# Attention's preparation in another order: keys by halves of the sequence, queries split ahead of the gathers, constants behind the first maximum

## The chip, the cores and the metric

The kernel runs on one core of a Trainium2 chip as a single program. The metric is the time of one execution on the device in microseconds (us); the lower the better. The engines of the core are named as the profile names them: PE (TensorE, matrix products and transposes), DVE (VectorE), ACT (ScalarE), POOL (GpSimd) and SP (SyncE, which here only issues DMA transfers). Each engine runs its own list of instructions strictly in order and waits on semaphores for the others.

## The reference, cut to what matters

The program is one step of a hybrid decoder layer: RMS norm, one input projection, attention beside a state-space model, an output projection and a convolutional feed-forward block. It is run for a prompt of 1024 positions and for 8 sample rows with 2048 cached positions each. The change touches the attention alone. For the prompt (8 heads, 2 key heads, head width 64, query blocks of 128) and the sample rows, three branches are computed and added with gates:

```python
s_c = jnp.einsum('bqhgd,bnhd->bqhgn', q, kv_c[:, :, 0]) * scale      # compressed keys
...
o_s = jnp.einsum('bqhgm,bqhmd->bqhgd', masked_softmax(s_s, m_s), v_s)  # selected blocks
...
o_w = jnp.einsum('bqhgw,bwhd->bqhgd', masked_softmax(s_w, m_w), v_w)   # window of 512
g = jax.nn.sigmoid(gate_logits)
return g[..., 0:1] * o_c + g[..., 1:2] * o_s + g[..., 2:3] * o_w
```

## The kernel before, in words

The program is a row of stages; `stage_attend` stands between `stage_compress` (compressed keys and values) and the state-space stage. It works through 16 groups: query block `i` (128 queries) times key head. For each group PE first makes scores only to find their maxima (a "look", lines 1242 and 1245, 1233 and 1234 for the compressed branch); DVE reduces them (`top`, line 1617), PE turns the maxima (line 1254), and DVE writes them into the lower rows of `q2` (line 1634), so that the real score (lines 1275, 1278, 1279) comes out with its maximum already taken off. ACT takes the exponential (line 1467), PE multiplies by the values (line 1293), ACT, PE and DVE bring the product back and weigh it with `gates` ("out"). Scores are computed in two parts: queries and keys are split into a rounded upper part (`q_up`, `k_up`, `kT` rows 0 to 63) and a rest (`q2` on POOL, line 1547; `kT` rows 64 to 127 on DVE, line 1577); `k2` holds the keys again (POOL, line 1495) and constants in its lower half (DVE, line 1597).

The order of the steps of all groups, with the steps of the sample rows woven in, is one list, `ORDER`, which every engine walks through; it is the same before and after. At its beginning stand both first splits, the three looks of group 0, their `merge` and `turn`, and then the first score. Twenty-odd steps later comes `("cmp weigh", 0)`, the first step of the sample rows that needs `grow`.

Ahead of that list each engine has a preparation of its own. PE turns keys and compressed values (lines 1194, 1197, 1200), then waits for the split keys, the compressed keys (`kc`, `kc2`) and the kept values. ACT computes `exp` of the gate logits, splits the four key quarters `c` (two branches by two halves of the sequence) and then splits the queries of groups 0 and 1. POOL copies the keys into `k2`, makes masks, issues the first five gathers (`fetch`, line 1530) and subtracts the queries' upper parts. DVE copies the values, makes `grow`, `rows4` and `qsm`, computes `gates` from the logits, and only then subtracts the keys' upper parts, sets constants and prepares `kc`.

`grow` are the gates of the 8 sample rows, one row of 3 numbers for each head of each sample row, brought by 64 small DMAs of SP. SP may start them when DVE has announced the gates (`gated`, second increment):

```python
sp.wait_ge(gated, 2)
sp.wait_ge(lanes_made, 1)
for b in range(NB):
    for h in range(NH):
        r = LANES * (b % (NB // 2)) + h
        sp.dma_start(k.grow[r:r + 1, b // (NB // 2), :], k.gates[b:b + 1, NT, 3 * h:3 * h + 3]).then_inc(grow_in, 16)
```

DVE waits for all of them in `cmp weigh` of the first half of the sample rows, ahead of lines 1604 and 1605:

```python
elif kind == "cmp weigh":
    dve.wait_ge(s_powered, order_of["cmp max", g] + 1)
    if g == 0:
        dve.wait_ge(grow_in, 16 * NB * NH)
    weight(0, g)
```

PE needs what DVE writes there in `cmp turn` (line 1322).

Of the kernel before, what the change touches and what calls it, by code (L numbers as in the profile page):

```python
# [949 lines left out]
def stage_attend(nc, k):  # L950
# [64 lines left out]
    k_split = nc.alloc_semaphore("k_split")  # L1015
# [33 lines left out]
    k.attend_sems = [v_turned, v_kept, gated, k_turned, k_upper, k_split, k2_rows, k2_const, kc_upper, kc_split, minus_made, masked,  # L1049
# [115 lines left out]
    TURN, ROW = 2, 3  # L1165

    with nc.Block() as block:
# [21 lines left out]
        def _(pe):  # L1189
            for c in range(4):  # L1190
                src = KVW * (1 + c // 2)
                for a in range(4):
                    t = 4 * (c % 2) + a
                    mm = pe.transpose(k.ps[:, c, a * P:a * P + P], k.kv[:, t, src:src + P], k.ident[:])
                mm.then_inc(k_turned, 1)
# [7 lines left out]
            pe.wait_ge(k_split, 16)  # L1203
            pe.wait_ge(kc_split, 3)
            pe.wait_ge(v_kept, 2)
# [16 lines left out]
            for step in ORDER:  # L1222
                kind, g, *rest = step
                i, kvh = GROUPS[min(g, len(GROUPS) - 1)]
                if kind == "look":
                    br, h0, nh, b_lo, b_hi = rest
                    if h0 == 0 and br == 0:
                        pe.wait_ge(q_upper, 2 * g + 2)
                    wait_bank(pe, looks)
# [27 lines left out]
                elif kind == "score":  # L1257
# [3 lines left out]
                    if br == SEL and b == 0:  # L1261

                        pe.wait_ge(q_rest, g + 1)
                        pe.wait_ge(reduced, looks_before[g] + 1)
                        if g == 0:
                            pe.wait_ge(k2_rows, 8)
                            pe.wait_ge(k2_const, 1)
                            pe.wait_ge(masked, 4)
# [12 lines left out]
                elif kind == "value":  # L1281
# [6 lines left out]
                    else:  # L1288
                        pe.wait_ge(v_set, 1)
                        pe.wait_ge(v_kept, 1)  # L1290
# [16 lines left out]
                elif kind == "cmp score":  # L1307
                    to_row(step)
                    if g == 0:
                        pe.wait_ge(s_const, 1)  # L1310
                    for bb in range(NH2):
# [78 lines left out]
        def _(act):  # L1390
            act.activation(k.glog[:, 0:NT], k.kv[:, 0:NT, 3 * KVW:], ACT.Exp, scale=-1.0)
            act.activation(k.glog[0:NB, NT], k.kv[0:NB, NT, 3 * KVW:], ACT.Exp, scale=-1.0).then_inc(gated, 1)
            for c in range(4):
                act.wait_ge(k_turned, c + 1)
                act.activation(k.k_up[:, c], k.ps[:, c, :], ACT.Copy).then_inc(k_upper, 1)
                act.wait_ge(k_upper, c + 1)
                for kvh in range(NKV):
                    act.activation(k.kT[0:HD, c // 2, kvh, 4 * P * (c % 2):4 * P * (c % 2 + 1)], k.k_up[HD * kvh:HD * (kvh + 1), c],
                                   ACT.Copy).then_inc(k_split, 1)
# [6 lines left out]
            def upper(g):  # L1406
# [4 lines left out]
                for half in range(2):  # L1411
                    act.activation(k.q_up[HD * half:HD * half + HD, g % 2], q_of(g), ACT.Copy).then_inc(q_upper, 1)
            scores = values = 0
            for step in ORDER:
                kind, g, *rest = step
                if kind == "split":
                    upper(g)
# [40 lines left out]
                elif kind == "score":  # L1458
# [6 lines left out]
                    if scores == 0:  # L1465
                        act.wait_ge(k2_rows, 8)
                    act.activation(probs[br][:, b - first].rearrange("p h q -> p (h q)"), k.ps[:, 4 + scores % 2, :], ACT.Exp,
# [12 lines left out]
        def _(pool):  # L1480
# [7 lines left out]
            pool.wait_ge(minus_made, 3)  # L1488
            pool.wait_ge(*k.rows_stored)
            pool.wait_ge(v_set, 1)  # L1490
            pool.wait_ge(gated, 1)
            for c in range(4):
                pool.wait_ge(k_upper, c + 1)
                for kvh in range(NKV):
                    pool.tensor_copy(k.k2[0:HD, c // 2, kvh, 4 * P * (c % 2):4 * P * (c % 2 + 1)],
                                     k.k_up[HD * kvh:HD * (kvh + 1), c].bitcast(F32)).then_inc(k2_rows, 1)
            pool.wait_ge(k2_rows, 8)
# [41 lines left out]
            for kind, g, *rest in ORDER:  # L1539
                if kind == "unit":  # L1540
                    fetch(g)
                elif kind == "split":
                    pool.wait_ge(q_upper, 2 * g + 2)
                    if g >= 2:

                        pool.wait_ge(scored, scores_to(g - 2, CMP))
                    pool.tensor_tensor(k.q2[0:HD, g % 2], q_of(g), k.q_up[0:HD, g % 2].bitcast(F32), ALU.subtract  # L1547
                                       ).then_inc(q_rest, 1)

        @block.vector  # L1550
        def _(dve):
            link = Link(dve, a_link)
            for br in range(2):
                v = KVW * (1 + br) + P
                dve.tensor_copy(k.v1[:, :, br, :, 0:HD], k.kv[:, 0:NT, v:v + P].rearrange("p t (h d) -> p t h d", h=NKV))
            dve.wait_ge(k.u_spilled, 16)
            dve.memset(k.grow[:], 0.0).then_inc(lanes_made, 1)
            for f in range(4):
                ins = dve.tensor_scalar(k.rows4[:, f], k.rows_of[:], 4.0, float(f), ALU.mult, ALU.add)
            ins.then_inc(lanes_made, 1)  # L1560
# [990 lines left out]
```

## Time and profile before

| what | value |
|---|---|
| time, median of 3 runs | 1937.73 us (1937.3 to 1938.95) |
| the profiled execution's own time | 1938.17 us |
| its span, first to last instruction | 1936.5 us |
| mean granted clock of PE | 0.951 |
| busy: PE, DVE, ACT, POOL | 92%, 47%, 29%, 16% of the span |

The attention stage lies at 384 to some 830 us of the span. Shares of busy time say which engine has most to do over the whole program; the change lies in the stage's first 50 us, so the rows that matter are the order of time and the waits there. "Idle before" in brackets is the time that an engine stood still ahead of an instruction, and behind the arrow what ended it.

### The profile page before, as it was taken

The page shows a single profiled execution, that of the slowest core. Times are in us where ns is not written, and L with a number is a line of the kernel's source. Part 1 is how long each engine was busy: PE and PEld are TensorE (multiplying, and loading weights), DVE is VectorE, ACT ScalarE, POOL GpSimd, SP SyncE. Part 2 cuts the span into 40 slices and gives each one's busy share as a digit, 9 for nine tenths or more (in the row PEclk, how much of TensorE's full clock was granted, in tenths as well). Part 3 has the DMA queues.
Part 4 walks back from the last instruction along what each step waited for, and adds up shares of the span by engine and source line. Part 5 has one row for each costly group of instructions (what it writes and reads, how often), then busy time and mean ns, then how long its engine had stood idle before and what let it go on. Part 6 is the DMA issues. An engine that isn't in the chain of part 4 may idle for free. (4 is left out here: it accounts for less than half of the span.)

```text
span 1936.5 us, 27098 instructions
## 1 busy us (share of the span) xinstructions
PE 1773.3 (92%) x10876; PEld 1496.6 (77%) x10876; DVE 908.3 (47%) x1408; ACT 565.1 (29%) x872; POOL 311.8 (16%) x273
## 2 busy tenths in 40 slices
PE   5999999949989999858879799999999999999988
PEld 4655989936555554456579789999999999999977
DVE  3366127755554444154031265555555555555454
ACT  4000115534443443212031242222322222232222
POOL 0000100032123111210021022222212222222110
PEclk8999999969999999968989799999999999999999
DMA  6222434312325233661020311111211211112102
GB/s 253 50 73 109 164 111 180 126 55 66 109 68 194 65 103 138 206 171 43 0 87 1 77 34 33 45 53 32 65 32 32 65 32 56 41 32 65 32 12 93
DMA packets 90956, 155.15 MB, mean 80 GB/s; under 512 B 15574, under 2 KB 68350, under 8 KB 88526
## 3 DMA queue, kind: packets, MB, share of 16 engines
q1 hardware_dynamic: 76976, 92.77, 14.8%
q0 software_dynamic: 13056, 59.77, 9.2%
q10 hardware_dynamic: 848, 1.54, 0.3%
q8 instruction: 54, 0.88, 0.2%
q14 instruction: 22, 0.18, 0.0%
HBM read 133.61 MB, written 24.83 MB: 82 GB/s over the span
## 5 line engine op out<-in xcount | busy, mean ns | idle before, releaser
L2240 PE MATMUL ps<-h_up,w_split 128*128 128x344 f32 x2112 | 403.5, 323 | 9.2 <-DVE h_rest L2410 7.3
L2419 DVE TENSOR_TENSOR xT<-ps,xT 128x1032 f32<-128x1032 f32 x176 | 216.9, 1233 | 326.5 <-PE ps L2240 326.5
L2240 PEld LDWEIGHTS ps<-h_up,w_split 128*128 128x128 f32 x2112 | 344.1, 189 | 20.6 <-issue 13.9
L2240 PE MATMUL ps<-gated,wd_split 128*128 128x344 f32 x1584 | 266.2, 324 | 3.0 <-POOL wd_split L2396 2.1
L2240 PEld LDWEIGHTS ps<-gated,wd_split 128*128 128x128 f32 x1584 | 250.2, 188 | 12.5 <-DVE xT L2419 8.0
L2240 PE MATMUL ps<-h_rest,w_split 128*128 128x344 f32 x1056 | 225.1, 322 | 0.0
L2240 PEld LDWEIGHTS ps<-h_rest,w_split 128*128 128x128 f32 x1056 | 179.5, 190 | 0.0
L2336 ACT ACTIVATE hu<-ps 128x1032 f32<-128x1032 f32 x44 | 45.4, 1033 | 342.5 <-PE ps L2240 342.5
L2426 DVE SCALAR_TENSOR_TENSOR cv<-hu,ccol,cv 128x1024 f32<-128x1024 f32 x88 | 135.0, 1534 | 16.4 <-ACT cv L2338 10.7
L2376 POOL TENSOR_TENSOR w_split<-w_raw,w_split 128x1024 fp32r<-128x1024 f32 x44 | 106.1, 2411 | 177.9 <-ACT w_split L2321 177.9
L1617 DVE TENSOR_REDUCE top<-ps 128x1 f32<-128x384 f32 (+4 forms) x124 | 71.3, 586 | 120.5 <-PE ps L1242 63.9
L433 PE MATMUL ps<-w_kvg,mixT 128*128 128x396 f32 (+1 forms) x288 | 96.8, 497 | 0.0
L1530 POOL DMA_INDIRECT unit<-in_cache_kv_sel,rows x64 | 60.4, 944 | 185.7 <-PE ps L1341 97.7
L1242 PE MATMUL ps<-kT,q_up 128*128 128x128 f32 (+3 forms) x336 | 74.5, 312 | 15.3 <-DVE kc L1594 10.7
L1242 PEld LDWEIGHTS ps<-kT,q_up 128*128 128x128 f32 x336 | 63.5, 207 | 30.7 <-issue 11.9
L2081 PE MATMUL ps<-mix_up,wo_split 128*128 128x344 f32 x384 | 74.0, 326 | 11.4 <-POOL wo_split L2111 11.4
L433 PEld LDWEIGHTS ps<-w_kvg,mixT 128*128 128x128 f32 (+1 forms) x288 | 51.2, 179 | 42.8 <-issue 7.8
L851 PE MATMUL ps<-rowsT,w_c 128*128 128x128 f32 (+1 forms) x576 | 81.2, 288 | 1.4 <-ACT rowsT L920 1.3
L2396 POOL TENSOR_TENSOR wd_split<-wd_raw,wd_split 128x1024 fp32r<-128x1024 f32 x22 | 54.9, 2496 | 168.3 <-ACT wd_split L2360 168.3
L1275 PE MATMUL ps<-q_up,kT 128*128 128x512 f32 x132 | 70.2, 532 | 12.4 <-POOL q L1547 9.9
L851 PEld LDWEIGHTS ps<-rowsT,w_c 128*128 128x128 f32 x576 | 74.9, 204 | 3.0 <-issue 3.0
L2081 PEld LDWEIGHTS ps<-mix_up,wo_split 128*128 128x128 f32 x384 | 63.4, 192 | 12.1 <-issue 11.9
(438 smaller groups left out, 2507.6 us busy)
## 6 DMA issues: line engine op xcount, KB each, us to landing
w_raw<-in_w_up SPq DMA_DIRECT2D x44, 512.0 KB, 5.5
wd_raw<-in_w_down SPq DMA_DIRECT2D x22, 512.0 KB, 3.5
unit<-in_cache_kv_win POOLq DMA_DIRECT2D x16, 512.0 KB, 4.2
x_kept<-xT SPq DMA_DIRECT2D x1, 4128.0 KB, 25.4
xT<-x_kept SPq DMA_DIRECT2D x1, 4128.0 KB
xtok<-in_x_prompt SPq DMA_DIRECT2D x2, 2048.0 KB, 8.0
w_qu<-in_w_in SPq DMA_DIRECT2D x2, 2048.0 KB, 8.7
w_out_sb<-in_w_out SPq DMA_DIRECT2D x4, 1024.0 KB, 5.0
```

The lines of the kernel that those rows point to most:

```text
L433: mm = pe.matmul(k.ps[0:n, bank + c, 0:KVH], hT[:, a, t * P:t * P + n], k.w_kvg[:, a, c * KVH:(c + 1) * KVH], **on)
L851: mm = pe.matmul(k.ps[:, 4 + 2 * (j % 2) + h, x * P:x * P + n], k.w_c[:, x, 2 * quad + a].rearrange("p r e -> p (r e)"), k.rowsT[:, f % 4, ...
L1242: mm = pe.matmul(out, k.q_up[:, g % 2, h0 + h, :], k.kT[:, br, kvh, b0 * P:(b0 + nb) * P], start=True, stop=b0 not in masks)
L1275: pe.matmul(out, first, k.q_up[:, g % 2].rearrange("p h q -> p (h q)"), start=True, stop=False)
L1530: pool.indirect_dma_start(unit, None, pages, bass.IndirectOffsetOnAxis(ap=k.rows4[:, f, NH2 * n + bb:NH2 * n + bb + 1], axis=0)).then_inc( ...
L1617: dve.tensor_reduce(to, s, AX.X, ALU.max).then_inc(reduced, 1)
L2081: mm = pe.matmul(k.ps[:, 4 * (d % 2) + c, 0:TG], k.wo_split[:, d % 2, wn, a, :], x[:, a, c * TG:c * TG + TG], start=(a == 0 and m == 0), s ...
L2240: mm = pe.matmul(k.ps[:, bank + c, 0:TG], w(wn), x(xn)[:, c * TG:c * TG + TG], start=start and m == 0, stop=stop and m == 2)
L2376: pool.tensor_tensor(k.w_split[:, z, 1], k.w_raw[:, z], k.w_split[:, z, 0].bitcast(F32), ALU.subtract).then_inc(w_rest, 1)
L2396: pool.tensor_tensor(k.wd_split[:, 1], k.wd_raw[:], k.wd_split[:, 0].bitcast(F32), ALU.subtract).then_inc(w_rest, 1)
L2419: dve.tensor_tensor(x, k.ps[:, bank:bank + 3, 0:TG], x, ALU.add).then_inc(added, 1)
L2426: dve.scalar_tensor_tensor(k.cv[:, z, 0:SEQ], k.hu[:, z, 1 - n:SEQ + 1 - n], w, k.cv[:, z, 0:SEQ], ALU.mult, ALU.add)
```

## The change

Nothing is computed otherwise; the preparation of the attention is put in another order, with semaphores to match.

- Keys: the four quarters are turned in the order 0, 2, 1, 3, so both branches' first half of the sequence come first. ACT, DVE and POOL split and copy the first half, then (ACT) the queries of group 0, then the second half. PE's first look waits for the first half only; the second half is waited for by the first group that needs it, `(4, 0)`, and by the sample rows' first score.
- Compressed keys and kept values: PE waits for them only at the first step that uses each.
- Queries: POOL subtracts the upper parts of groups 0 and 1 ahead of the masks and of the gathers instead of behind the five gathers.
- Constants: `grow`'s zeros, `rows4`, `qsm`, `gates`, the rests of the second half's keys and the constants of `k2`'s second half become a function `constants()`, which DVE calls behind the `turn` of group 0.
- Gate logits: ACT first copies them out, and takes their `exp` behind the second query split.

```diff
-            for c in range(4):
+            for n, c in enumerate(CUTS):
...
-            pe.wait_ge(k_split, 16)
-            pe.wait_ge(kc_split, 3)
-            pe.wait_ge(v_kept, 2)
+            pe.wait_ge(k_first, 4)
+            pe.wait_ge(k_rest, 4)
...
+                    if h0 == 0 and br == 0 and g == HALF:
+                        pe.wait_ge(k_first, 8)
+                        pe.wait_ge(k_rest, 8)
+                    if br == CMP and g == 0:
+                        pe.wait_ge(kc_split, 3)
...
+            take_keys(0, CUTS[0])
+            take_keys(1, CUTS[1])
+            upper(0)
+            take_keys(2, CUTS[2])
+            take_keys(3, CUTS[3])
...
+            upper(1)
+            act.wait_ge(g_copied, 1)
+            act.activation(k.glog[:, 0:NT], k.glog[:, 0:NT], ACT.Exp, scale=-1.0)
+            act.activation(k.glog[0:NB, NT], k.glog[0:NB, NT], ACT.Exp, scale=-1.0).then_inc(gated, 1)
...
+            key_rows(0, CUTS[0])
+            key_rows(1, CUTS[1])
+            rest_of(0)
...
+            key_rows(2, CUTS[2])
+            key_rows(3, CUTS[3])
+            rest_of(1)
...
+            def constants():
+
+                dve.memset(k.grow[:], 0.0).then_inc(lanes_made, 1)
+                for f in range(4):
+                    ins = dve.tensor_scalar(k.rows4[:, f], k.rows_of[:], 4.0, float(f), ALU.mult, ALU.add)
+                ins.then_inc(lanes_made, 1)
+                link(dve.memset(k.qsm[:], 0.0))
...
+                dve.wait_ge(gated, 1)
+                link(dve.tensor_scalar(k.glog[:, 0:NT], k.glog[:, 0:NT], 1.0, None, ALU.add))
...
+                dve.reciprocal(k.gates[:, 0:NT], k.glog[:, 0:NT])
+                link(dve.reciprocal(k.gates[0:NB, NT], k.glog[0:NB, NT]))
+                dve.sem_inc(gated, 1)
...
+                rest_of_keys(2, CUTS[2])
+                rest_of_keys(3, CUTS[3])
+                tops_rows(1)
+            rest_of_keys(0, CUTS[0])
+            dve.memset(k.q2[HD:P].bitcast(F32), 0.0).then_inc(kc_upper, 1)
+            rest_of_keys(1, CUTS[1])
...
+            tops_rows(0)
...
                     looks += 1
+                    if g == 0:
+                        constants()
```

DVE's list at the beginning of the stage, before (names: `kv` is the projected rows, `v_3223` is `v1`, the values, `glog` the gate logits, `kT` the split keys):

```order
L1555 COPY v_3223<-kv 128x8x2x64 x2
L1557 MEMSET grow 128x6
L1559 TENSOR_SCALAR rows_3253<-rows_of 128x8 x4
L1561 MEMSET qsm 128x256
L1564 COPY qsm<-qT 64x8x4 x2
L1567 TENSOR_SCALAR glog<-glog 128x192
L1568 TENSOR_SCALAR glog<-glog 8x24
L1569 RECIPROCAL gates<-glog 128x192
L1570 RECIPROCAL gates<-glog 8x24
L1572 TENSOR_SCALAR gates<-gates,seen_cmp 128x8
L1577 TENSOR_TENSOR kT<-ps,k_up 64x512 x8
```

In the changed kernel the same instructions stand behind the three reductions and the write of the first maxima:

```order
L1671 TENSOR_REDUCE top<-ps 128x4 x3
L1688 TENSOR_TENSOR q_3222<-ps,each_3220 12x512
L1613 MEMSET grow 128x6
L1615 TENSOR_SCALAR rows_3253<-rows_of 128x8 x4
L1617 MEMSET qsm 128x256
L1620 COPY qsm<-qT 64x8x4 x2
L1623 TENSOR_SCALAR glog<-glog 128x192
L1624 TENSOR_SCALAR glog<-glog 8x24
L1625 RECIPROCAL gates<-glog 128x192
L1626 RECIPROCAL gates<-glog 8x24
L1628 TENSOR_SCALAR gates<-gates,seen_cmp 128x8
L1602 TENSOR_TENSOR kT<-ps,k_up 64x512 x4
```

So `gates`, which stood ahead of the key rests, now stand behind the write of the first `turn`. What DVE does ahead of that `turn` in the changed kernel is this:

```order
L1595 COPY v_3223<-kv 128x8x2x64 x2
L1602 TENSOR_TENSOR kT<-ps,k_up 64x512 x2
L1633 MEMSET q_3222 64x1024
L1602 TENSOR_TENSOR kT<-ps,k_up 64x512 x2
L1640 MEMSET vc_3216 128x2
L1641 MEMSET kc 128x256
L1642 MEMSET kc_3215 128x256
L1645 CAST kc<-kcp 64x2x64
L1646 CAST kc_3215<-kcp 64x2x64
L1648 TENSOR_TENSOR kc<-kcp,kc 64x2x64
L1650 CAST kc_3215<-minus 64x256
L1607 CAST k_3213<-minus 64x2x512 x2
```

Half of the key rests and half of `k2`'s constants are left in it. POOL's list from its first key copy to its first gather, in the changed kernel (`k_3213` is `k2`, `q_3222` is `q2`; before, all 8 copies came first and both subtractions stood behind five gathers):

```order
L1520 CAST k_3213<-k_up 64x512 x4
L1530 TENSOR_TENSOR q_3222<-qT,q_up 64x512
L1540 MEMSET mask_cmpT 128x1024
L1541 MEMSET each_3220 128x4
L1543 AFFINE_SELECT mask_cmpT<-mask_cmpT 128x1024
L1546 AFFINE_SELECT each_3220<-each_3220 128x4 x3
L1520 CAST k_3213<-k_up 64x512 x4
L1530 TENSOR_TENSOR q_3222<-qT,q_up 64x512
```

The subtraction for group 0 moved from behind the gathers to behind four key copies.

## Rows read from the trace of the kernel before

**Rows 1.** Waits of 384 to 460 us: who waited for whom, total, times, longest.

```profile
PE ps L1242 <- DVE kc L1594: 10.7, 1, 10.7
...
PE ps L1275 <- POOL q L1547: 9.9, 1, 9.9
...
DVE ss L1604 <- DMA grow<-gates: 1.0, 1, 1.0
```

**Rows 2.** PE in order of time: start, length, instruction, idle time before.

```profile
384.44 3.05 PE L1194 MATMUL ps<-ident,kv 128*128 128x128 f32 x16 [2.40 <-PEq L814]
...
398.85 0.45 PE L1242 MATMUL ps<-kT,q_up 128*128 128x128 f32 x1 [10.65 <-DVE kc L1594]
...
404.17 0.38 PE L1254 MATMUL ps<-ident,top 128*12 128x128 f32 x1 [0.57 <-DVEq L1624]
...
414.45 0.80 PE L1275 MATMUL ps<-q_up,kT 128*128 128x512 f32 x1 [9.90 <-POOL q L1547]
...
420.00 0.26 PE L1233 MATMUL ps<-kc,q_up 128*128 128x64 f32 x1
...
433.70 0.49 PE L1322 MATMUL ps<-ident,pcs 128*127 128x128 f32 x2
```

**Rows 3.** The tile `grow`: its DMAs, length min/median/max, first and last start.

```profile
L1176 SPq DMA_DIRECT2D grow<-gates x64: 619/620/757, 388.8 to 430.8; - x64
```

**Rows 4.** DVE in order of time.

```profile
385.68 0.06 DVE L1557 MEMSET grow<- 128x6 f32 x1
...
389.17 5.73 DVE L1577 TENSOR_TENSOR kT<-ps,k_up 64x512 fp32r<-64x512 f32 x8
...
395.07 0.27 DVE L1584 MEMSET kc<- 128x256 f32 x1
...
395.87 0.91 DVE L1586 MEMSET q<- 64x1024 f32 x1 [0.25 <-issue]
396.81 0.51 DVE L1589 CAST kc<-kcp 64x128 fp32r<-64x128 f32 x1
...
398.67 2.77 DVE L1597 CAST k<-minus 64x2048 fp32r<-64x2048 f32 x2
401.47 1.29 DVE L1617 TENSOR_REDUCE top<-ps 128x4 f32<-128x512 f32 x2
403.63 0.42 DVE L1617 TENSOR_REDUCE top<-ps 128x4 f32<-128x256 f32 x1 [0.87 <-PE ps L1234]
405.80 0.68 DVE L1634 TENSOR_TENSOR q<-ps,each 12x512 fp32r<-12x512 f32 x1 [1.74 <-POOL each L1504]
...
432.46 0.17 DVE L1604 RECIPROCAL ss<-ss 128x1 f32<-128x1 f32 x1 [0.98 <-DMA grow<-gates]
```

**Rows 5.** ACT in order of time.

```profile
386.19 0.60 ACT L1395 ACTIVATE k_up<-ps 128x512 fp32r<-128x512 f32 x1
...
388.01 0.57 ACT L1395 ACTIVATE k_up<-ps 128x512 fp32r<-128x512 f32 x1
...
395.56 2.59 ACT L1412 ACTIVATE q_up<-qT 64x512 fp32r<-64x512 f32 x4
```

**Rows 6.** POOL in order of time.

```profile
402.64 0.95 POOL L1498 MEMSET mask_cmpT<- 128x1024 bf16 x1
...
404.84 0.85 POOL L1504 TENSOR_SCALAR_AFFINE_SELECT each<-each 128x4 f32<-128x4 f32 x3
...
413.12 2.50 POOL L1547 TENSOR_TENSOR q<-qT,q_up 64x512 fp32r<-64x512 f32 x2
```

**Rows 7.** Line 1495 on POOL: length in ns, min/median/max.

```profile
L1495 POOL CAST k<-k_up x8: 602/610/1698, 395.3 to 402.0; 64x512 fp32r<-64x512 f32 x8
```

**Rows 8.** Busy time by stretch: PE, PEld, DVE, ACT, POOL, then granted clock, DMA.

```profile
414.40:422.60 8.20, 8.15 (x34) 6.31 (x35) 1.81 (x3) 1.19 (x2) 1.22 (x1) 0.50 0.34 134
...
436.20:439.70 3.50, 3.50 (x12) 2.20 (x11) 0.68 (x1) 1.46 (x3) 0.77 (x1) 0.51 0.00 0
```

**Rows 9.** PE's waits from 446 to 800 us: total, times, longest.

```profile
PE ps L1368 <- DMA unit<-in_cache_kv_sel,rows: 5.0, 2, 3.7
```

More of the change, by code:

```diff
@@ L1390, in _, with take_keys, upper @@
         def _(act):
[L1391 to L1396, printed above, removed]
-                for kvh in range(NKV):
-                    act.activation(k.kT[0:HD, c // 2, kvh, 4 * P * (c % 2):4 * P * (c % 2 + 1)], k.k_up[HD * kvh:HD * (kvh + 1), c],
-                                   ACT.Copy).then_inc(k_split, 1)
+            act.activation(k.glog[:, 0:NT], k.kv[:, 0:NT, 3 * KVW:], ACT.Copy)
+            act.activation(k.glog[0:NB, NT], k.kv[0:NB, NT, 3 * KVW:], ACT.Copy).then_inc(g_copied, 1)
+            def take_keys(n, c):
+                act.wait_ge(k_turned, n + 1)
+                act.activation(k.k_up[:, c], k.ps[:, n, :], ACT.Copy).then_inc(k_upper, 1)
+                act.wait_ge(k_upper, n + 1)
+                for kvh in range(NKV):
+                    act.activation(k.kT[0:HD, c // 2, kvh, key_half(c)], k.k_up[HD * kvh:HD * (kvh + 1), c],
+                                   ACT.Copy).then_inc(k_first, 1)
+            def upper(g):
+                if g >= 2:
+                    act.wait_ge(scored, scores_to(g - 2, CMP))
+                for half in range(2):
+                    act.activation(k.q_up[HD * half:HD * half + HD, g % 2], q_of(g), ACT.Copy).then_inc(q_upper, 1)
+            take_keys(0, CUTS[0])
[3 more added lines that the diff above has]
+            take_keys(3, CUTS[3])
             act.wait_ge(v_turned, 1)
@@ L1404, in _ @@
             act.activation(k.knT[:].rearrange("p a b -> p (a b)"), k.ps[:, 6, 2 * P:2 * P + 2 * NB], ACT.Copy).then_inc(v_kept, 1)
-            def upper(g):
-                if g >= 2:
-                    act.wait_ge(scored, scores_to(g - 2, CMP))
-                for half in range(2):
-                    act.activation(k.q_up[HD * half:HD * half + HD, g % 2], q_of(g), ACT.Copy).then_inc(q_upper, 1)
+            upper(1)
+            act.wait_ge(g_copied, 1)
+            act.activation(k.glog[:, 0:NT], k.glog[:, 0:NT], ACT.Exp, scale=-1.0)
+            act.activation(k.glog[0:NB, NT], k.glog[0:NB, NT], ACT.Exp, scale=-1.0).then_inc(gated, 1)
             scores = values = 0
@@ L1416, in _ @@
                 if kind == "split":
-                    upper(g)
+                    if g >= 2:
+                        upper(g)
                 elif kind == "cmp exp":
@@ L1541, in _ @@
                     fetch(g)
[L1542 to L1548, printed above, removed]
+                elif kind == "split" and g >= 2:
+                    rest_of(g)
         @block.vector
@@ L1554, in _ @@
                 v = KVW * (1 + br) + P
[L1555 to L1560, printed above, removed]
-            link(dve.memset(k.qsm[:], 0.0))
-            for kvh in range(NKV):
-                hs = slice(kvh * GQA, (kvh + 1) * GQA)
-                ins = dve.tensor_copy(k.qsm[HD * kvh:HD * kvh + HD, :, hs], k.qT[:, hs, SEQ:TOK].rearrange("d h b -> d b h"))
@@ L1573, in _, with rest_of_keys @@
[L1573 to L1574 removed]
+                ins = dve.tensor_copy(k.v1[:, :, br, :, 0:HD], k.kv[:, 0:NT, v:v + P].rearrange("p t (h d) -> p t h d", h=NKV))
+            ins.then_inc(v_copied, 1)
+            def rest_of_keys(n, c):
+                dve.wait_ge(k_upper, n + 1)
                 for kvh in range(NKV):
                     rows = slice(HD * kvh, HD * (kvh + 1))
[L1577 to L1578 removed]
@@ L1579, in _, with tops_rows @@
-            dve.memset(k.v1[:].rearrange("p t b h d -> p (t b h) d")[:, :, HD:HD + 1], 1.0)
+                    dve.tensor_tensor(k.kT[HD:P, c // 2, kvh, key_half(c)], k.ps[rows, n, :], k.k_up[rows, c].bitcast(F32),
+                                      ALU.subtract).then_inc(k_rest, 1)
+            def tops_rows(half):
+                for br in range(2):
+                    ins = dve.tensor_copy(k.k2[HD:P, br, :, 4 * P * half:4 * P * (half + 1)],
+                                          k.minus[HD:P, br:br + 1].unsqueeze(2).broadcast_to([HD, NKV, 4 * P]))
+                ins.then_inc(k2_const, 1)
@@ L1595, in _ @@
                             ).then_inc(kc_split, 1)
-            for br in range(2):
-                ins = dve.tensor_copy(k.k2[HD:P, br].rearrange("p h n -> p (h n)"),
-                                      k.minus[HD:P, br:br + 1].broadcast_to([HD, NKV * SEQ]))
-            ins.then_inc(k2_const, 1)
+            tops_rows(0)
+            dve.memset(k.v1[:].rearrange("p t b h d -> p (t b h) d")[:, :, HD:HD + 1], 1.0).then_inc(v_set, 1)
             looks = outs = looked_at = 0
```

83 lines of the change are left out of this document (49 added, 34 removed).

## The prediction

> **What bounds the kernel now.** I read the list of waits of the stage's beginning first, then each engine's instructions there in order of time. PE, the engine with the most to do, stands still twice at the start: 10.7 us until DVE has prepared the compressed keys, and 9.9 us until POOL has subtracted the queries [rows 1]. The first look starts at 398.85 and the first score at 414.45 [rows 2], so some 30 us pass between the last of the key turns (384.44 and 3.05 long) and the first score. That is what the change is aimed at, and taken alone it would pay.
>
> The list has a third entry, small and easily passed over: DVE waits 1.0 us for `grow` [rows 1]. It shows that a second chain arrives at the same time: `gates` on DVE, then 64 transfers that SP issues one behind the other, of 0.62 us each, the first at 388.8 and the last at 430.8 [rows 3], so one every 0.667 us (42.0 over 63), then DVE at 432.46 [rows 4]. From the first issue to DVE's release are 43.7 us (432.46 − 388.8). DVE runs in order, so everything behind `cmp weigh` waits with it, and PE's `cmp turn` at 433.70 [rows 2] takes what DVE writes there. So before, two chains meet at 432.5: the look-and-score chain, 1.0 us early, and the chain of `grow`. Shortening only the first gains at most 1.0 us; what delays the second delays all that follows.
>
> **What the change does to the first chain.** I replay it from the rows. The first four of PE's 16 turns are done about 385.2. ACT has no `exp` ahead any more, so its first upper part starts about 385.4; a quarter costs it 1.82 us (388.01 − 386.19) [rows 5]. Two quarters end at 389.0, and group 0's queries (half of 2.59) at 390.3. PE can look from there, 8.5 us earlier than at 398.85.
>
> DVE sees the first upper part at 386.0. Then, all from [rows 4]: two key rests of 0.72 (5.73 over 8) to 387.5, the zeros of `q2` 0.91 to 388.4, two more rests to 389.8, the zeros of `kc` and `kc2` 0.8 with the gap behind them (395.87 − 395.07) to 390.6, the `kc` work 1.86 (398.67 − 396.81) to 392.5, half of the constants of `k2` (1.39 of 2.77) to 393.9, with the values' ones 394.0. The third reduction starts 2.16 behind the first (403.63 − 401.47), at 396.2, and ends at 396.6; PE's turn takes 0.38 and a semaphore [rows 2] to 397.1; DVE's write of the maxima 0.68 to 397.8. That write needs POOL's masks too. POOL starts when PE has turned all, about 388.2 (387.5 and, as an estimate, 0.7 for the four small turns behind): four copies at the median of 0.61 [rows 7], one subtraction (half of 2.50) and 3.05 for the masks (from 402.64 to the end of the row at 404.84) [rows 6], done at 394.9: in time. So the first score starts about 398, some 16.5 us earlier than before.
>
> Then comes `constants()`: as much of it as stood ahead of the first key rest took 3.5 us (389.17 − 385.68); four key rests 2.9 and the other half of `k2`'s constants 1.4 make 7.8, to 405.6. DVE's next reduction is queued behind it, and PE's look into the compressed keys of group 1, which needs that bank, comes at 406.3 and not at 420.0 [rows 2]: 13.7 us are still won. DVE would then be at `cmp weigh` at 417.8 (432.46 − 1.0 − 13.7).
>
> **What it does to the second chain.** `gates` are now computed behind the first `turn`. From the zeros of `grow` to SP's first issue were 3.1 us (388.8 − 385.68) [rows 3, 4]. From 397.8 that makes 400.9 and not 388.8: 12.1 us later. ACT's `exp`, which `gates` wait for, stands behind the second queries: 389.0 and 1.3, two more quarters 3.6, the kept values, the second queries 1.3 and the `exp` with its table, done before 398.5, when DVE reaches it. SP has nothing else in its queue; its 64 issues cover 42 us whatever the other engines do: they ran from 388.8 to 430.8 beside idle and full stretches with 757 ns as the longest [rows 3]. So the last lands, and DVE goes on, at 400.9 + 43.7 = 444.6. The 13.7 us won become a wait of about 27 us on DVE (444.6 − 417.8), with PE standing before `cmp turn` for nearly as long.
>
> **The sum.** The place where both chains meet moves from 432.5 to 444.6: +12.1 us. Behind it the order is the same on every engine, and what is fetched or turned there is released by the stage's own steps, so the shift goes through to the end. What the earlier preparation gives (16.5 at the first score) counts nothing, since the wait covers it.
>
> To this comes PE's clock. After the 9.9 us of idling ahead of 414.45 PE ran at a granted clock of 0.50, the lower level of 1.2 GHz, for the 8.2 us to 422.6; in a later stretch, from 436.2, it was 0.51 for 3.5 us [rows 8]. With 25 us of idling ahead of `cmp turn` I expect the longer stretch at that place: up to 4.7 us more at the lower level. Half of such time is lost at most, 2.4; DVE's and ACT's steps between don't slow down, so the least is 0. I take the middle, 1.2.
>
> The Trainium skill (TensorE: Matmul & The Clock Gate, Terms) puts the penalty of throttled time at that time multiplied by one minus the granted share, which is the whole 2.4 us; by it the sum would be 1.2 us higher. No row here shows the same work at both levels back to back.
>
> Sum: 12.1 + 1.2 = 13.3 on the profiled execution's 1938.17 us: 1951.5. That execution lies 0.4 above the median of the runs, so for a median I say 1951.0.
>
> Unpriced parts: the two new copies of the logits take the place of the `exp` on the same tiles, and DVE's and POOL's instructions are the same but for two halves each of the `k2` constants. Cut in halves these may cost up to a few tenths more; it lies in the range.
>
> **Rivals.**
> (a) The gates come later still, because DVE and POOL hinder each other ahead of the first maximum. Line 1495's copies took 602 to 1698 ns [rows 7]. With all four at the longest, POOL's masks are done at 399.3 (388.2 + 6.8 + 1.25 + 3.05), the write of the maxima starts there and not at 397.1, and each us goes through: +2.2, 1953.2. Against it: the median is 610. The Trainium skill (SBUF — State Buffer, SBUF: two separate sides) describes a port pair that VectorE and GpSimd hold in turn, one blocking the other; the spread in rows 7 agrees with it, and by it this rival would be the likelier the more of DVE's casts fall beside the copies.
> (b) Other side: the 64 transfers don't hold up DVE, since they run closer together than before. DVE must be through by 432.46 for no change; first issue at 400.9 and 1.7 us from the last issue to the release (432.46 − 430.8) leave 29.9 for 63 steps, 0.47 us a step. At 0.25 a step (63 steps and 1.7 end at 418) the wait would vanish, and the end would move by the 13.7 and the 1.0 of the old wait: 1923.5. Against it: not one of the 64 took under 619 ns [rows 3].
> (c) The shift is given back behind the meeting point, where PE waits for something that the late start doesn't delay. Between 446 and 800 PE waits 5.0 us for gathers [rows 9]; if those landed early against PE, 1946.0. Against it: each is issued when PE frees its buffer, so it moves along.
>
> **How the numbers follow.** Forecast (12.1 and 0 to 2.4 for the clock, with 1 us either way for the replay): 0.76, by itself 1948.5 to 1953.5. (a) 0.11, (b) with smaller gains of its kind 0.06, (c) 0.05, and 0.02 for a recovery that ends within 0.2% (3.9 us, about what a measurement of this kernel can tell from no change). The range 1947.5 to 1955.0 takes in the forecast, (a) and the smaller cases of (c), and leaves out some 0.15. Faster by over 0.2%: 0.06; within: 0.02; slower: 0.92.
>
> **What the profile of the changed kernel would show.** Right: a first look about 390.5 and a first score about 398; SP's `grow` transfers from about 401 to 443, 0.62 us each; DVE's wait for `grow` grown from 1.0 to some 27 us and ended near 444.6; PE idle some 25 us before `cmp turn`; a stretch of granted clock 0.5 behind it; the rest of the stage shifted alike. Wrong: if the transfers start at 390, or if the wait for `grow` stays at a few us, the sum falls, and the time goes under 1938. If the wait is there but the end is shifted by less than 8 us, (c) holds.

## The result, and the profile after

| | before | after |
|---|---|---|
| time, median of 5 runs | 1937.73 us (1935.03 to 1938.95) | 1957.55 us (1950.2 to 1958.57) |
| ratio of the runs, 95% interval | | 1.0081 (1.0058 to 1.0104) |
| the profiled execution's own time | 1938.17 us | 1953.14 us |

The kernel became slower by 0.8%, well over the 0.2% that can be told from no change. The ratio isn't the quotient of the two medians, which is 1.0102 and lies within its interval. Times 1937.73 the ratio is 1953.4 us, inside the predicted range, but the interval goes from 1949.0 to 1957.9 us, and the median of these five runs lies 2.6 us above the range's upper end. Six more runs of the same kernel (experiment 7) had a median of 1954.59 and a ratio of 1.0079.

The first line of the page after:

```profile
span 1951.4 us, 27112 instructions
```

The waits of 384 to 460 us after, answering [rows 1] (total, times, longest):

```profile
DVE ss L1658 <- DMA grow<-gates: 24.9, 1, 24.9
...
PE ps L1337 <- DVE pcs L1728: 24.1, 1, 24.1
...
PE ps L1245 <- DVE top L1671: 5.8, 2, 2.9
...
PE ps L1254 <- ACT q_up L1423: 3.4, 1, 3.4
```

Both waits at which the change was aimed are gone: PE's 10.7 us for `kc` and 9.9 us for POOL's queries. The third line of [rows 1], 1.0 us, has become the first here, 24.9 us, and PE stands 24.1 us behind it.

PE after in order of time, answering [rows 2]:

```profile
381.40 1.94 PE L1202 MATMUL ps<-ident,kv 128*128 128x128 f32 x16 [2.40 <-PEq L814]
...
387.22 0.45 PE L1254 MATMUL ps<-kT,q_up 128*128 128x128 f32 x1 [3.40 <-ACT q_up L1423]
...
396.30 0.77 PE L1287 MATMUL ps<-q_up,kT 128*128 128x512 f32 x1 [0.82 <-DVE q L1688]
...
404.86 0.42 PE L1245 MATMUL ps<-kc,q_up 128*128 128x64 f32 x1 [2.83 <-DVE top L1671]
...
444.11 0.80 PE L1337 MATMUL ps<-ident,pcs 128*127 128x128 f32 x2 [24.11 <-DVE pcs L1728]
...
465.36 0.66 PE L1356 MATMUL ps<-ident,unit 128*128 128x128 f32 x4 [0.16 <-ACT vcs L1456]
```

This execution reached the attention stage 3.0 us earlier than the one before (381.40 against 384.44), for a reason in an earlier stage (last section). So places are compared by their distance from the first key turn, S. The first look lies 5.8 behind S and not 14.4, the first score 14.9 and not 30.0, the look into the compressed keys of group 1 23.5 and not 35.6. `cmp turn` lies 62.7 behind S and not 49.3.

The tile `grow` after (length min/median/max in ns, first and last start), answering [rows 3]:

```profile
L1184 SPq DMA_DIRECT2D grow<-gates x64: 619/620/757, 399.4 to 441.4; - x64
```

The transfers have the same three lengths to the nanosecond and the same 42.0 us from first to last start; they only begin 18.0 behind S and not 4.4.

DVE after in order of time, answering [rows 4]:

```profile
387.36 1.15 DVE L1645 CAST kc<-kcp 64x128 fp32r<-64x128 f32 x1
...
388.44 1.04 DVE L1646 CAST kc<-kcp 64x128 fp32r<-64x128 f32 x1
...
389.82 1.09 DVE L1650 CAST kc<-minus 64x256 fp32r<-64x256 f32 x1
...
390.84 1.29 DVE L1607 CAST k<-minus 64x1024 fp32r<-64x1024 f32 x2
...
395.52 0.68 DVE L1688 TENSOR_TENSOR q<-ps,each 12x512 fp32r<-12x512 f32 x1 [0.53 <-PE ps L1266]
...
396.27 0.06 DVE L1613 MEMSET grow<- 128x6 f32 x1
...
443.06 0.16 DVE L1658 RECIPROCAL ss<-ss 128x1 f32<-128x1 f32 x1 [24.94 <-DMA grow<-gates]
```

POOL beside the three casts, in order of time:

```profile
387.16 1.26 POOL L1530 TENSOR_TENSOR q<-qT,q_up 64x512 fp32r<-64x512 f32 x1 [0.47 <-ACT q_up L1423]
388.38 1.02 POOL L1540 MEMSET mask_cmpT<- 128x1024 bf16 x1
...
389.67 1.10 POOL L1543 TENSOR_SCALAR_AFFINE_SELECT mask_cmpT<-mask_cmpT 128x1024 bf16<-128x1024 bf16 x1
```

The three casts of the `kc` work end at 388.51, 389.48 and 390.91; the three instructions of POOL end at 388.42, 389.40 and 390.77. Each cast ends 0.08 to 0.14 us behind the POOL instruction that was running beside it. From the first cast to the first constants of `k2` pass 3.48 us (390.84 − 387.36), against 1.86 before [rows 4].

Busy time by stretch after (PE, PEld, DVE, ACT, POOL, then granted clock, DMA), answering [rows 8]:

```profile
443.10:454.80 11.70, 9.19 (x29) 5.77 (x30) 6.14 (x18) 2.06 (x4) 0.00 (x0) 0.50 0.00 0
...
454.80:460.00 5.20, 5.20 (x42) 4.12 (x41) 3.64 (x15) 2.27 (x4) 0.00 (x0) 1.00 0.01 3
```

From the release on the granted clock is at 0.50, the lower level, for 11.7 us. Before, the stretch at that level in this place was 3.5 us long and began 3.7 us behind the release [rows 8].

PE's waits from 446 to 810 us after, answering [rows 9]:

```profile
PE ps L1383 <- DMA unit<-in_cache_kv_sel,rows: 5.0, 2, 3.7
```

It is the same 5.0 us, to the digit: the later start gave nothing back there.

Two more places measure the rest of the stage: the first turn of a gathered unit, and the first turn of `oacc`, which begins the next stage. PE before:

```profile
452.60 0.66 PE L1341 MATMUL ps<-ident,unit 128*128 128x128 f32 x4
...
827.20 1.51 PE L1738 MATMUL ps<-ident,oacc 128*128 128x128 f32 x6 [1.77 <-PEq L1167]
```

PE after:

```profile
844.09 1.30 PE L1794 MATMUL ps<-ident,oacc 128*128 128x128 f32 x5 [1.77 <-PEq L1175]
```

With R for DVE's release (432.46 and 443.06), G for the gathered unit and E for `oacc`, the 14.9 us by which the span grew are: −3.0 ahead of S, +13.6 from S to R, +2.2 from R to G, +4.1 from G to E, and −2.0 behind E. The first, the fourth and the last of these go with the time that the granted clock was at 0.50 in the two executions: 13.6 us less of it ahead of S, 8.6 us more from G to E, 12.2 us less behind E.

### The profile page after: what moved, and what is told of

It reads as the page before. It is cut to its first block and busy times, and to the rows that moved or that the text cites. A ratio compares the mean times of both kernels' runs of the same rounds, so it can differ in the third digit from the quotient of the medians.

```text
span 1951.4 us, 27112 instructions
## 1 busy us (share of the span) xinstructions
PE 1772.3 (91%) x10876; PEld 1490.0 (76%) x10876; DVE 908.4 (47%) x1410; ACT 565.9 (29%) x874; POOL 310.7 (16%) x273
## 3 DMA queue, kind: packets, MB, share of 16 engines
q1 hardware_dynamic: 76976, 92.77, 14.7%
## 5 line engine op out<-in xcount | busy, mean ns | idle before, releaser
L2296 PEld LDWEIGHTS ps<-h_up,w_split 128*128 128x128 f32 x2112 | 343.0, 188 | 22.2 <-issue 14.7
L2482 DVE SCALAR_TENSOR_TENSOR cv<-hu,ccol,cv 128x1024 f32<-128x1024 f32 x88 | 133.3, 1515 | 16.4 <-ACT cv L2394 10.7
L2137 PE MATMUL ps<-mix_up,wo_split 128*128 128x344 f32 x384 | 74.0, 326 | 11.3 <-POOL wo_split L2167 11.3
L851 PE MATMUL ps<-rowsT,w_c 128*128 128x128 f32 (+1 forms) x576 | 76.3, 276 | 1.6 <-ACT rowsT L920 1.3
L851 PEld LDWEIGHTS ps<-rowsT,w_c 128*128 128x128 f32 x576 | 69.9, 192 | 3.4 <-issue 3.4
```

Of the source, the lines that this page charges most:

```text
L851: mm = pe.matmul(k.ps[:, 4 + 2 * (j % 2) + h, x * P:x * P + n], k.w_c[:, x, 2 * quad + a].rearrange("p r e -> p (r e)"), k.rowsT[:, f % 4, ...
L2137: mm = pe.matmul(k.ps[:, 4 * (d % 2) + c, 0:TG], k.wo_split[:, d % 2, wn, a, :], x[:, a, c * TG:c * TG + TG], start=(a == 0 and m == 0), s ...
L2296: mm = pe.matmul(k.ps[:, bank + c, 0:TG], w(wn), x(xn)[:, c * TG:c * TG + TG], start=start and m == 0, stop=stop and m == 2)
L2482: dve.scalar_tensor_tensor(k.cv[:, z, 0:SEQ], k.hu[:, z, 1 - n:SEQ + 1 - n], w, k.cv[:, z, 0:SEQ], ALU.mult, ALU.add)
```

## The experiments

The theory: `grow`'s 64 transfers cost 43.7 us from the first issue, whatever runs beside them, and the change starts them later by what DVE now does ahead of `gates`; that alone is the loss. The rivals: the preparation's new order itself loses the time (contention of DVE and POOL, later steps), or the low clock behind the wait does. All kernels compute the same unless it is said otherwise.

**1. The changed kernel with `gates` first.** ACT takes the `exp` at once, DVE calls `constants()` ahead of the key rests, and only the second half's rests stay behind the first `turn`.

```diff
-            act.activation(k.glog[:, 0:NT], k.kv[:, 0:NT, 3 * KVW:], ACT.Copy)
+            act.activation(k.glog[:, 0:NT], k.kv[:, 0:NT, 3 * KVW:], ACT.Exp, scale=-1.0)
...
+            def second_half():
                 rest_of_keys(2, CUTS[2])
                 rest_of_keys(3, CUTS[3])
                 tops_rows(1)
+            constants()
             rest_of_keys(0, CUTS[0])
...
-                        constants()
+                        second_half()
```

> The changed kernel, but the gates are made at the front again: ACT takes the exp of the logits first, DVE makes grow's zeros, rows4, qsm and gates ahead of the key rests; the second half's rests and constants stay behind the first maximum. Theory (the 64 transfers of grow start behind gates and hold up DVE for as much longer as gates came later): the transfers start 4 to 5 us behind the stage's first instruction, as before the change; DVE's wait for grow falls from 24.9 to 6 to 12 us; the time goes back to that of the kernel before, 1935 to 1942, and not below by more than 3 us, because the transfers still need 43.7 us. Rival (the loss comes from the new order of keys and queries, or from what still stands behind the first maximum): the time stays above 1946.

Measured: 1941.29 us (12 runs, 1935.4 to 1947.42), ratio 1.0020 (1.0005 to 1.0035). Its `grow` transfers:

```profile
L1184 SPq DMA_DIRECT2D grow<-gates x64: 619/620/757, 387.6 to 429.6; - x64
```

Its wait on DVE:

```profile
431.26 0.16 DVE L1658 RECIPROCAL ss<-ss 128x1 f32<-128x1 f32 x1 [12.24 <-DMA grow<-gates]
```

With the issue back at its old place the loss is nearly gone, and what the preparation won earlier stands as a wait of 12.2 us (just over the expected 6 to 12) in front of the same transfers. All other parts of the new order are still in this kernel, so they aren't the loss. The 0.2% that is left isn't lost at the meeting place, since R lies 48.0 behind S in both kernels; where it lies wasn't traced.

**2. The changed kernel with nine transfers.** One store of the sample rows' gates to memory, and then eight loads, each of 8 heads by 3 numbers.

```diff
+            sp.dma_start(k.grow_kept, k.gates[0:NB, NT, :]).then_inc(grow_in, 16)
+            sp.wait_ge(grow_in, 16)
             for b in range(NB):
-                for h in range(NH):
-                    r = LANES * (b % (NB // 2)) + h
-                    sp.dma_start(k.grow[r:r + 1, b // (NB // 2), :], k.gates[b:b + 1, NT, 3 * h:3 * h + 3]).then_inc(grow_in, 16)
+                r = LANES * (b % (NB // 2))
+                sp.dma_start(k.grow[r:r + NH, b // (NB // 2), :], k.grow_kept[b].rearrange("(h z) -> h z", z=3)).then_inc(grow_in, 16)
```

> The changed kernel, with grow brought by 9 transfers instead of 64 (gates to memory once, then one for each sample row). Theory: from the first issue to the release about 10 us instead of 43.7, so grow lands near 410, ahead of the 417.7 at which DVE comes to it; the wait vanishes, and what the new preparation won early comes through: 13 to 16 us under the kernel before, 1921 to 1926. Rival (the wait only moves elsewhere, or the loss has another cause): above 1935.

Measured: 1927.25 us (5 runs, 1927.15 to 1928.29), ratio 0.9947 (0.9927 to 0.9967). Its transfers:

```profile
L1182 SPq DMA_DIRECT2D grow_kept<-gates x1: 269/269/269, 401.7 to 401.7; - x1
...
L1186 SPq DMA_DIRECT2D grow<-grow_kept x8: 263/295/297, 404.7 to 407.0; - x8
```

DVE at `cmp weigh`:

```profile
419.74 0.16 DVE L1660 RECIPROCAL ss<-ss 128x1 f32<-128x1 f32 x1
```

DVE no longer waits there: 36.7 behind S, against 48.0 before and 61.7 after. That settles the cause: with the transfers short, the new order is worth 0.5%, and this kernel beats both. The size was missed: some 10 us were gained, not 13 to 16. DVE arrived 36.7 behind S where the replay had 33.4 (417.8 − 384.44).

**3. The kernel before with nine transfers.** The same edit in the kernel before.

```diff
+            sp.dma_start(k.grow_kept, k.gates[0:NB, NT, :]).then_inc(grow_in, 16)
+            sp.wait_ge(grow_in, 16)
...
-                for h in range(NH):
```

> The kernel before, with the same 9 transfers. Theory (two chains met there within 1 us): DVE's wait of 1.0 us for grow goes away and no more than that is won, 1934 to 1938. Rival (the 64 transfers cost the kernel before as well, by SP or by contention): more than 5 us under it, below 1932.

Measured: 1935.94 us (12 runs, 1932.85 to 1942.18), ratio 0.9987 (0.9971 to 1.0004). DVE at `cmp weigh`:

```profile
428.91 0.16 DVE L1606 RECIPROCAL ss<-ss 128x1 f32<-128x1 f32 x1
```

The wait is gone, and R lies 47.5 behind S and not 48.0. By the runs it was worth little (0.0013 of 1937.7 are 2.5 us, with no change in the interval). With the reordering the same edit is worth some 26 us (1.0081 − 0.9947 of 1937.7): the two chains had ended together, and neither could gain alone.

**4. The changed kernel with PE kept at work in the wait.** 100 products, thrown away, ahead of the first `cmp turn`.

```diff
                 elif kind == "cmp turn":
                     to_turn(step)
+                    if g == 0:
+                        for _n in range(100):
+                            pe.matmul(k.ps[:, TURN, :], k.kT[:, 0, 0, 0:P], k.kT[:, 0, 0, 0:4 * P], start=True, stop=True)
```

> The changed kernel with 100 added matrix products on PE ahead of the first cmp turn, where it stands idle for 24 us, into a bank that this step writes anyway; their results are thrown away. Theory (of the 14.97 us by which the changed kernel's profiled span is longer, 10.6 are the release of DVE, and the rest is PE's clock behind the idle time and chance in other stages): the granted clock stays at 1.0 through the wait, the 10 us at 0.5 behind it go away, the release stays where it is, and the time falls by 2 to 4 us, to 1949 to 1954. Rival (the clock costs nothing there): no change, and the granted clock behind the wait is of no consequence.

Measured: 1958.97 us (5 runs, 1954.26 to 1961.59), ratio 1.0106 (1.0082 to 1.0130). The time didn't fall, and the expected 1949 to 1954 was missed. From R to G were 19.8 us where the changed kernel took 22.3, so the place itself did go faster; experiment 8 takes this up.

**5. The kernel before with `gates` late.** Nothing of the reordering but this: the block from `grow`'s zeros to `gates` moved behind the `turn` of group 0.

```diff
-            dve.memset(k.grow[:], 0.0).then_inc(lanes_made, 1)
...
+            def constants():
+                dve.memset(k.grow[:], 0.0).then_inc(lanes_made, 1)
...
                     looks += 1
+                    if g == 0:
+                        constants()
```

> The kernel before with one part of the change alone: grow's zeros, rows4, qsm and gates move behind the first turn on DVE; keys, queries, masks and gathers stay as they were. The first turn is written at about 405 (POOL's masks come 1.3 us sooner), gates are ready 3.1 us later, near 408 and not 388.8. Theory (what counts is when the 64 transfers may start): release and end 18 to 25 us later than before, 1956 to 1963. Rival (the loss needs the new order of keys and queries): within 5 us of the kernel before.

Measured: 1960.79 us (5 runs, 1957.71 to 1967.1), ratio 1.0110 (1.0088 to 1.0132). Its transfers:

```profile
L1177 SPq DMA_DIRECT2D grow<-gates x64: 619/620/757, 409.1 to 451.0; - x64
```

DVE at `cmp weigh`:

```profile
452.70 0.16 DVE L1608 RECIPROCAL ss<-ss 128x1 f32<-128x1 f32 x1 [21.21 <-DMA grow<-gates]
```

This one part of the change, alone, brings a loss of the same kind. It is larger than the change's, since the transfers start later still, 24.1 behind S and not 18.0. Together with experiment 1 it shows the part to be both enough and needed.

**6. The changed kernel with POOL held until `kc` is split.** It tells whether POOL is what slows DVE's casts.

```diff
             pool.wait_ge(v_turned, 1)
+            pool.wait_ge(kc_split, 3)
             key_rows(0, CUTS[0])
```

> The changed kernel, but POOL starts its key copies only when DVE has prepared the compressed keys. Looked at for one thing, DVE's four casts into kc, kc2 and the first half of k2, which took 1.15, 1.04, 1.09 and (two) 1.29 us beside POOL's copies. If the two engines hinder each other, the first three take 0.3, 0.25 and 0.4 us or less. If not, they stay near 1.1. The time itself tells nothing, since POOL's masks are late then.

Measured, in one execution: 1954.88 us. DVE's `kc` work:

```profile
387.22 0.22 DVE L1646 CAST kc<-kcp 64x128 fp32r<-64x128 f32 x1
387.36 0.21 DVE L1647 CAST kc<-kcp 64x128 fp32r<-64x128 f32 x1
387.60 0.28 DVE L1649 TENSOR_TENSOR kc<-kcp,kc 64x128 fp32r<-64x128 f32 x1
387.92 0.29 DVE L1651 CAST kc<-minus 64x256 fp32r<-64x256 f32 x1
388.13 1.71 DVE L1608 CAST k<-minus 64x1024 fp32r<-64x1024 f32 x2
```

With POOL standing still the same casts take 0.22, 0.21 and 0.29 us, and the whole piece 0.91 where it took 3.48 beside POOL's subtraction and masks (not its key copies, as the expectation has it). The kernel isn't faster for it: POOL's masks come later, DVE's write of the maxima with them (it ends 15.5 behind S, not 14.8), from `grow`'s zeros to the first issue pass some 5.0 us and not 3.17, and the release lies 64.1 behind S, not 61.7. So the contention is shown, as a part of where `gates` lie, and holding POOL back is no remedy.

**7. The changed kernel once more**, unaltered, beside experiment 8.

> The changed kernel unaltered, on the chip on which the next one runs. 1950 to 1959, as it was; the profile shows whether the stretch of granted clock 0.5 behind the release has the same 10 us.

Measured: 1954.59 us (6 runs, 1950.87 to 1957.18), ratio 1.0079 (1.0059 to 1.0099). The stretch behind the release:

```profile
444.00:455.90 11.90, 9.57 (x32) 6.15 (x32) 5.99 (x17) 2.27 (x5) 0.00 (x0) 0.50 0.00 0
```

It is 11.9 us long here, after 11.7 in the first execution.

**8. Experiment 4 once more.** The same kernel beside experiment 7, to see whether its missing gain was chance.

> The changed kernel with the 100 added matrix products, on the same chip as the unaltered one. If the clock behind the wait sets the end, it is 2 to 4 us faster than the unaltered one. If what is won there is lost again later in the stage or by chance in the others, within 2 us of it.

Measured: 1958.48 us (5 runs, 1956.09 to 1962.67), ratio 1.0103 (1.0080 to 1.0126). The added products on PE:

```profile
426.19 22.85 PE L1337 MATMUL ps<-kT 128*128 128x512 f32 x100
```

The stretches behind the release and in an earlier stage that no kernel here changes:

```profile
453.30:456.70 3.40, 2.96 (x7) 1.59 (x7) 0.98 (x2) 0.59 (x1) 0.00 (x0) 0.50 0.00 0
...
284.00:299.00 15.00, 15.00 (x81) 15.00 (x81) 4.47 (x14) 4.03 (x15) 0.97 (x1) 0.50 0.73 275
```

With PE at work, the low clock behind the release lasts 3.4 us as before, R to G is 19.7 us and not 22.5, and the whole stage from S to E is 3.0 us shorter than in experiment 7 (458.5 against 461.5). The program is no shorter, because S lies at 387.9 and not at 381.9: in both executions of this kernel the low clock took a stretch at 282 us, and in both of the unaltered one it didn't. The low clock behind the wait is thus a cost of 2 to 3 us in this kernel; why the earlier stretch went with the added products isn't settled by two executions of each.

**9. Nine transfers, and the second half's key rests later still.** It asks whether experiment 2 leaves some of the replayed gain behind `constants()`: the rests move behind group 1's look into the window.

```diff
+            def second_half():
                 rest_of_keys(2, CUTS[2])
                 rest_of_keys(3, CUTS[3])
                 tops_rows(1)
...
                     looks += 1
+                    if g == 1 and br == WINDOW:
+                        second_half()
```

> The changed kernel with 9 transfers for grow, and DVE's constants in two pieces: gates and the like behind the first turn as in the change, the second half's key rests and constants (4.3 us) behind the second reduction of group 1. PE's look into the compressed keys of group 1, which waited 3.1 us for DVE's reductions, is then made while DVE does the second piece. If that wait is on the path now, 1 to 2 us are won over the 1927.3 us of the version with 9 transfers: 1925 to 1927. If DVE's work is what counts and not its place, the wait turns up at the next turn or at the sample rows' first score and the time stays at 1926.5 to 1928.5.

Measured: 1926.24 us (7 runs, 1919.24 to 1935.6), ratio 0.9937 (0.9913 to 0.9962), which can't be told from experiment 2. PE's looks into the compressed keys of groups 0 and 1:

```profile
398.25 0.39 PE L1247 MATMUL ps<-kc,q_up 128*128 128x64 f32 x1 [4.72 <-DVE top L1675]
...
406.90 0.26 PE L1247 MATMUL ps<-kc,q_up 128*128 128x64 f32 x1
```

The clock in two stretches that follow:

```profile
407.00:410.00 3.00, 2.58 (x12) 1.55 (x10) 2.91 (x5) 0.98 (x2) 1.89 (x2) 0.50 0.96 316
410.00:424.00 14.00, 12.05 (x53) 6.97 (x53) 6.31 (x19) 3.52 (x8) 1.25 (x1) 0.50 0.24 89
```

In experiment 2 PE waits 3.1 us at each of the two looks. The wait at group 1's, at which the edit was aimed, is gone; the one at group 0's, ahead of all that the edit moves, is 4.7 us in this execution. A part turns up again where the expectation's second case has it: PE waits 1.7 us at group 1's turn (L1268, 411.26), since DVE's third reduction now stands behind the second piece. And the clock stays at the lower level to 430.6, where in experiment 2 it was up again from 411.3, and R lies 38.4 behind S and not 36.7. Whether the edit is worth anything stays open.

The distances in the profiled executions, in us (S the first key turn, R DVE's first use of `grow`, G the first turn of a gathered unit, E the next stage), by R − S:

| kernel | S | R − S | G − R | E − G | E − S |
|---|---|---|---|---|---|
| 2, nine transfers | 383.0 | 36.7 | 20.3 | 377.7 | 434.7 |
| 9, and rests later | 385.8 | 38.4 | 20.9 | 378.3 | 437.6 |
| 3, before, nine transfers | 381.4 | 47.5 | 20.3 | 376.1 | 443.8 |
| before | 384.4 | 48.0 | 20.1 | 374.6 | 442.8 |
| 1, `gates` first | 383.2 | 48.0 | 20.3 | 376.4 | 444.7 |
| after | 381.4 | 61.7 | 22.3 | 378.7 | 462.7 |
| 7, after again | 381.9 | 61.9 | 22.5 | 377.1 | 461.5 |
| 8, products in the wait | 387.9 | 62.5 | 19.7 | 376.2 | 458.5 |
| 4, products in the wait | 387.5 | 62.6 | 19.8 | 376.3 | 458.7 |
| 6, POOL held | 381.3 | 64.1 | 19.6 | 377.2 | 460.9 |
| 5, before, `gates` late | 385.0 | 67.7 | 20.6 | 377.8 | 466.1 |

From the first row to the last the release moves by 31.0 us and the stage grows by 31.4: what delays DVE at `grow` goes through to the end of the stage one for one, within the 4 us by which E − G differs.

## Why the prediction was right

**The meeting of two chains held.** The wait of 1.0 us for `grow` was the row that decided. With the first chain shortened and the second delayed, DVE waits 24.9 us (predicted: about 27) and PE 24.1 (25). Experiments 1 and 5 show that the place of `gates` alone makes the loss, experiment 2 that the rest of the reordering pays once the transfers are short. One sentence of the prediction is off: shortening only the first chain gains nothing, since DVE already waits for the transfers (experiment 1: R − S is 48.0, as before). The 1.0 us belongs to the second chain, and experiment 3 won 0.5 of it. And its "some 30 us" run from the first of the key turns to the first score; from the last they are 27. Neither enters its sum.

**The replay of the first chain held in its front part.** The first look was to come 8.5 us earlier and came 8.6 earlier by distance from S; the first score 16.5, and came 15.1; group 1's look 13.7, and came 12.1. The end was optimistic: DVE free of `grow` was to be at `cmp weigh` 14.7 us earlier, and experiment 2 measures 11.3 (48.0 − 36.7). Of the 3.4 us, 1.6 are lost before group 1's look, and 1.8 behind it: from that look on PE was at the lower level for another 2.6 us in the kernel before and for another 5.5 us in the changed one. The same two products, before at a granted clock of 1.00 and after at 0.50:

```profile
422.66 1.02 PE L1293 MATMUL ps<-prob_sel,v 128*65 128x512 f32 x2
...
407.71 1.92 PE L1305 MATMUL ps<-prob_sel,v 128*65 128x512 f32 x2
```

The replay had no term for the clock. This end of it counted nothing in the sum, since the wait covers it, but it set the size that experiment 2 missed.

**The 12.1 us of the transfers' later start measured 13.6.** They began 18.0 behind S, against 4.4. Of its two pieces the one from `grow`'s zeros to the first issue was right (3.17 us, taken as 3.1), and the 43.7 us from the first issue to the release are 43.6. Mis-sized was the way of DVE to the write of the maxima: it ended 14.8 behind S and not 13.4. The replay took the `kc` work at the 1.86 us of [rows 4]; it took 3.48, since three casts lay beside POOL. The 1.86 themselves weren't the price of the casts alone, which is 0.91 (experiment 6): before, they lay beside POOL's key copies, of some 0.61 us each [rows 7]. This is rival (a)'s mechanism, smaller than its 2.2 us and at another place: it wasn't POOL that was held up with its masks, and beside DVE's casts ran its subtraction and its masks, not its key copies. It came on top of the forecast and didn't replace it. The Trainium skill (SBUF — State Buffer, SBUF: two separate sides) says that of an instruction of VectorE that uses the shared port pair, as a cast can, and one of GpSimd the one that starts first holds the pair for its whole length while the other is blocked. The trace agrees: each cast ends 0.08 to 0.14 us behind POOL's instruction, and in experiment 6, without POOL, none takes over 0.29 us.

**The clock's 1.2 us measured 2.2**, at the upper part of the range of 0 to 2.4. That it fell within the range is luck in part. The low stretch lasted 11.7 us, 8.2 longer than the one of 3.5 in [rows 8]; at most 4.7 more had been expected, and half of 8.2 would be 4.1. And the 4.7 came from a misreading: the 8.2 us at 0.50 in [rows 8] weren't begun by the 9.9 us of idling, for the clock was at that level before and during it, as these two stretches of the kernel before show:

```profile
398.00:404.50 6.50, 4.72 (x25) 4.18 (x25) 5.12 (x7) 0.14 (x1) 6.12 (x7) 0.50 0.00 0
404.50:414.40 9.90, 0.05 (x1) 0.00 (x0) 0.68 (x1) 0.00 (x0) 7.80 (x17) 0.50 0.50 154
```

Behind a wait of DVE of nearly the same length (24.6 to 25.9 us) 3.4 us at the lower level make 19.7 us from R to G (experiment 8), 6.0 make 19.6 (experiment 6), and 11.9 make 22.5 (experiment 7). So 8.5 us more cost 2.8, and the cost isn't in proportion to the time. PE was busy for 9.57 of the 11.9 us, and the steps of DVE and ACT between don't slow down (DVE's L1706 takes 0.42 us at either level). The Trainium skill (TensorE: Matmul & The Clock Gate, Terms) has the penalty as the throttled time multiplied by one minus the granted share, by which 8.5 us at 0.50 would cost 4.2. The measurement is lower there; between experiments 6 and 7, where 5.9 us more cost 2.9, it agrees.

**Nothing was given back later.** Rival (c) falls with [rows 9], the same 5.0 us after, and with the one for one of the table. Rival (b) falls with the 64 transfers, none shorter than 619 ns. The 4.1 us by which the rest of the stage was longer had no term in the prediction. In eleven executions E − G lay between 374.6, which is before's, and 378.7, which is after's; the same kernel had 377.1 a second time. It goes with the clock: the four executions with 18.9 to 21.1 us at the lower level from G to E took 374.6 to 376.4, the seven with 25.6 to 31.9 us took 376.1 to 378.7. What decides how long the clock is low there stays open. That the profiled executions differ by 14.97 us, so near the forecast 13.3, is thus luck in part: the two pieces that the sum speaks of came to 15.8, and the others, −3.0, +4.1 and −2.0, happen to cancel nearly.

## What to carry to other kernels

When a list of waits shows a long one and, at the same time, a short one on another engine, follow the short one back to its source before shortening the long one: here its source was a row of 64 small transfers that take 42 us from whenever they may start. Move what starts such a row forward, never back, or cut the row down first: nine transfers turned this change from 0.8% slower into 0.5% faster, and did next to nothing without it. When an instruction's duration is carried to a new place, ask what runs beside it there; 1.86 us of casts became 3.48, and 0.91 where nothing did.

## What the runs showed of the hardware that was not expected

- Transfers of 12 bytes from one partition to another take SP 619 to 757 ns each, one every 0.667 us, with the same minimum, median and maximum in the kernels before and after and in experiments 1, 4, 5, 6 and 8 (in experiment 7 the longest took 758). Eight transfers of 96 bytes from memory took 263 to 297 ns, one every 0.33 us ((407.0 − 404.7) / 7).
- After nearly the same 24 us of idling on PE, the clock stayed at the lower level from the release on for 11.7 and 11.9 us in two executions of the changed kernel, and for 6.0 in experiment 6:

```profile
445.40:451.40 6.00, 3.46 (x7) 1.87 (x8) 3.59 (x11) 0.55 (x1) 0.00 (x0) 0.50 0.00 0
```

- In an earlier stage that is the same in every kernel, the clock falls at about 282 us in four of the eleven executions (before and experiments 4, 5 and 8, for 13.6 to 17.1 us), at 300.9 us in one (experiment 9, for 6.8 us), and not at all in the other six. The attention starts at 384.4 to 387.9 in the first five and at 381.3 to 383.2 in the six. Before, at 0.50:

```profile
284.00:296.00 12.00, 12.00 (x65) 12.00 (x65) 3.53 (x11) 3.54 (x11) 0.97 (x1) 0.50 0.69 264
```

After, at 1.00:

```profile
284.00:296.00 12.00, 10.84 (x102) 10.49 (x102) 7.44 (x26) 5.79 (x17) 0.97 (x1) 1.00 0.66 254
```

What decides it there isn't settled; it makes single executions of these kernels differ by some us, so that stages are better compared from their own beginning.
